# The gates' projection moved from the projection stage into the long convolution, and the late modulation rows moved the other way, in one layer of a hybrid Hyena / attention / expert block

## What is computed

```
mod_x = silu(c) @ w_mod + b_mod                    # 6 x 1024 columns; mod_c likewise for context
hx = modulate(rmsnorm(x), sh1, sc1);  hc likewise  # the first 2 x 1024 columns of mod
zx = hx @ w_in + b_in                              # 1024 x 5120
#   columns: hyena 3 x 512 | q 512 | k 512 | v 512 | gates 2 x 1024
kc, vc = hc @ w_in[k and v columns]                # context keys and values
v, x1, x2 = short_conv(hyena columns)
y = x1 * long_conv(v, filter 0);  hy = x2 * long_conv(y, filter 1)
na = neighbourhood_attention(q, k, v, kc, vc)
mix = (sigmoid(g_hy) * (hy @ w_branch_hy) + sigmoid(g_na) * (na @ w_branch_na)) @ w_out
x = x + g1 * mix                                   # the late 4 x 1024 columns of mod: g1, sh2, sc2, g2
x = x + g2 * expert_ffn(modulate(rmsnorm(x), sh2, sc2));  out = rmsnorm(x) * final_g
```

## Time and profile before

| | |
|---|---|
| median of 3 runs | 3085.92 us (3085.8, 3085.92, 3089.4) |
| the profiled execution's own time | 3089.23 us |
| its span, first to last instruction | 3087.4 us |
| mean granted TensorE clock | 0.953 of full |
| projection stage, PE's first to last matmul | 93.4 to 573.5 us |
| attention | about 578 to 829 us |
| long convolution | 829 to 1259 us |
| merge, output projection, routing | 1259 to about 1540 us |
| experts | the rest |
| busy share of the span | PE 91%, DVE 71%, ACT 50%, POOL 2% |

### The profile page before, as it was taken

The page is one execution under the profiler, slowest core; times in us unless marked ns, Lnnn a source line. Parts: engine busy times, 40 slices in busy tenths (PEclk is TensorE's granted clock), DMA queues, the critical chain, the costliest instruction groups (busy, mean ns, idle before and its releaser), DMA issues.

```text
span 3087.4 us, 34727 instructions
## 1 busy us (share of the span) xinstructions
PE 2815.9 (91%) x13273; PEld 2231.1 (72%) x13273; DVE 2180.7 (71%) x2132; ACT 1550.3 (50%) x1580; POOL 71.0 (2%) x35
## 2 busy tenths in 40 slices
PE   7899999788888994789399999999999999999997
PEld 2688888688644442568278888888888888888885
DVE  4341001376449999646698888888888988888887
ACT  4321122366421110112177777777777777777774
POOL 0000000000000000000000000000000000000000
PEclk8899999899899997899599999999999999999999
DMA  5223112522112221343399999999999999999995
GB/s 211 68 88 106 59 62 88 113 56 54 38 48 65 66 72 51 124 156 125 144 378 377 370 371 388 387 383 374 370 378 394 383 376 371 370 386 390 380 374 201
DMA packets 168042, 709.60 MB, mean 230 GB/s; under 512 B 28937, under 2 KB 66161, under 8 KB 100259
## 3 DMA queue, kind: packets, MB, share of 16 engines
q1 hardware_dynamic: 163444, 691.53, 59.3%
q0 software_dynamic: 4464, 16.25, 2.0%
HBM read 667.59 MB, written 40.14 MB: 229 GB/s over the span
## 4 chain that ended last, share of the span: by engine, by line
PE 46%; ACT 2%; issue 2%; DVE 1%; DMA 0%; DVEq 0%; ACTq 0%; POOLq 0%
PE moe_ps_gate L1827 15%; PE moe_ps_y L1817 14%; PE moe_ps_up L1827 14%; ACT moe_w_hi L1868 1%; PE moe_ps_h L1798 1%; PE moe_ps_x L1790 0%; DVE raw L1986 0%; ACT moe_xt_hi L1861 0%; DVE moe_h L1937 0%; ACT moe_sl L1879 0%; DMA moe_xe<-h_d,idx_col 0%; DVE raw L1973 0%; PE moe_ps_gate L1851 0%; PE moe_ps_gate L1853 0%; PE moe_ps_up L1851 0%
## 5 line engine op out<-in xcount | busy, mean ns | idle before, releaser
L1918 DVE TENSOR_TENSOR moe_w_lo<-raw,moe_w_hi 128x2048 fp32r<-128x2048 f32 x528 | 1207.5, 2291 | 156.9 <-ACT moe_w_hi L1868 156.9
L1868 ACT ACTIVATE moe_w_hi<-raw 128x2048 fp32r<-128x2048 f32 x528 | 1010.4, 1919 | 340.1 <-PE moe_ps_gate L1827 126.0
L1827 PE MATMUL moe_ps_gate<-moe_w_hi,moe_xt_hi 128*128 128x512 f32 (+1 forms) x768 | 288.8, 376 | 5.0 <-DVE moe_w_lo L1918 5.0
L1827 PE MATMUL moe_ps_up<-moe_w_hi,moe_xt_hi 128*128 128x512 f32 (+1 forms) x768 | 292.9, 381 | 0.0
L1827 PE MATMUL moe_ps_up<-moe_w_hi,moe_xt_lo 128*128 128x512 f32 (+1 forms) x768 | 286.6, 373 | 0.0
L1827 PE MATMUL moe_ps_up<-moe_w_lo,moe_xt_hi 128*128 128x512 f32 (+1 forms) x768 | 286.4, 373 | 0.0
L1827 PE MATMUL moe_ps_gate<-moe_w_hi,moe_xt_lo 128*128 128x512 f32 (+1 forms) x768 | 286.1, 373 | 0.0
L1827 PE MATMUL moe_ps_gate<-moe_w_lo,moe_xt_hi 128*128 128x512 f32 (+1 forms) x768 | 285.6, 372 | 0.0
L560 DVE TENSOR_TENSOR proj_w_lo<-w_in,proj_w_hi 128x2048 fp32r<-128x2048 f32 x20 | 45.7, 2290 | 275.6 <-ACT proj_w_hi L472 275.6
L1817 PE MATMUL moe_ps_y<-moe_w_hi,moe_ht_hi 128*128 128x512 f32 x704 | 218.7, 392 | 0.0
L1817 PE MATMUL moe_ps_y<-moe_w_lo,moe_ht_hi 128*128 128x512 f32 x704 | 217.1, 390 | 0.0
(11 more groups left out here) (269 smaller groups left out, 4321.9 us busy)
## 6 DMA issues: line engine op xcount, KB each, us to landing
raw<-in_w_moe SPq DMA_DIRECT2D x528, 1024.0 KB, 7.1
w_in<-in_w_in SPq DMA_DIRECT2D x20, 1024.0 KB, 5.7
hyena_w_mod<-in_w_mod SPq DMA_DIRECT2D x16, 1024.0 KB, 5.3
norm_w_mod<-in_w_mod SPq DMA_DIRECT2D x4, 2048.0 KB, 13.1
g_d<-proj_stage SPq DMA_DIRECT2D x16, 512.0 KB, 2.6
merge_gate<-g_d SPq DMA_DIRECT2D x16, 512.0 KB, 4.5
u_d<-proj_conv SPq DMA_DIRECT2D x12, 512.0 KB, 2.9
attn_k_raw<-qk_d SPq DMA_DIRECT2D x16, 320.0 KB, 6.0
```

Of the source, the lines that this page charges most:

```text
L1827: mm = pe.matmul(ps, hp[:, e % 2, k, :], wp[:, r, :], start=(k == 0 and x == 0), stop=(k == KD - 1 and x == 2))
L1868: act.activation(w_hi[:, g % PARTS], raw[:, g % RAW], ACT.Copy).then_inc(hi_ready, 1)
L1918: dve.tensor_tensor(w_lo[:, g % PARTS], raw[:, g % RAW], w_hi[:, g % PARTS].bitcast(F32), ALU.subtract).then_inc(lo_ready, 1)
```

## The change

1. **Projection.** Only 12 units are projected (hyena, q, k, v). The loops are unrolled. For the gates' 2048 columns the stage only makes the parts: 16 blocks of 128 columns are loaded (0.5 MB each), split by ACT and DVE into high and low, and stored to DRAM (`gw_d`, 1 MB each); the split input is stored too (`hq_d`, 8 transfers of 1 MB, right at the stage's start). Two blocks go with each of units 0 to 7.
2. **v** is projected for both units at once in matmuls of 512 columns for token tiles 2 to 9 (24 per tile); tiles 0 and 1 stay at 256 columns. The bias matmul goes; DVE evacuates with an addition of a bias row.
3. **Late modulation rows.** The 8 chunks are made in units 1 to 8 of the projection. For each, four quarters (0.5 MB, two slots) are loaded, and DVE folds them into one 128x512 tile with 8 operations (`fold`); one PE matmul with a column of ones sums over the partitions after the unit's own matmuls; DVE adds `b_mod` in the next unit; SP stores the row, waits for that store, and loads the next `b_mod` row into the same tile, ahead of the next quarters. Only row 0 (the latent's) is made.
4. **Long convolution.** Where `ps_mod` stood, PE runs `gates(n)`: 64 blocks (16 column blocks x 4 token quarters) of 24 fp32r matmuls of 256 columns. How many go with each of the 16 steps is a table, SHARE. POOL's queue loads the weight parts for each block anew (1 MB, two slots) and the input's quarter every 16 blocks (2 MB, one slot). ACT applies the sigmoid, SP stores 128 KB per block. The PSUM ring of `seg`/`turn`/`input` has 2 banks, not 3.
5. **Attention** stores its output to DRAM (`na_d`, 4 x 0.5 MB, the last one after the last block, with a wait), and the merge loads it (2 MB). DVE's own-step semaphores of all stages become one.

Cut to its core. SP's new order first (`chunk(u)` is u - 1 for units 1 to 8; `load_mod` waits for the fold of the quarter in its slot, `load_b_mod` for the store in `keep_mod`, `keep_mod` for the row, `keep_block` for DVE's low part), then PE's, DVE's, and the convolution's:

```diff
+                load_b_mod(0)
+                load_mod(0, 0)
+                load_mod(0, 1)
+                for q in range(T // QUARTER):
+                    for x, h in enumerate((h_hi, h_lo)):
+                        sp.dma_start(a["hq_d"][q][:, x], h[:, :, q * QUARTER:(q + 1) * QUARTER].bitcast(F32)
+                                     ).then_inc(keep["kept"], 16)
+                for u in range(SEG_V[0]):
+                    load(u + 2)
+                    n = chunk(u)
+                    if n:
+                        keep_mod(n - 1)
+                        load_b_mod(n)
+                        load_mod(n, 0)
+                        load_mod(n, 1)
+                    for c in range(CH_UNIT):
+                        if u < N_BLOCKS // 2:
+                            keep_block(2 * u + c)
+                            load_block(2 * u + c + 2)
+                        if n is not None:
+                            load_mod(n, 2 + c)
+                        keep_unit(u, c)
```

```diff
+                for u in range(SEG_V[0]):
+                    pe.wait_ge(lo_ready, u + 1)
+                    latents(u)
...
+                    if n is not None:
+                        pe.wait_ge(mod_used, 4 * n + 4)
+                        pe.wait_ge(mod_row_ready, MOD_EARLY + n)
+                        pe.matmul(ps_mod[0:1, :], ones[:], folded[:], start=True, stop=True).then_inc(mod_done, 1)
```

```diff
+                for u in range(SEG_V[0]):
+                    split(u + 1)
+                    n = chunk(u)
+                    if n:
+                        add_b_mod(n - 1)
+                    for c in range(CH_UNIT):
+                        if u < N_BLOCKS // 2:
+                            split_block(2 * u + c)
+                        if n is not None:
+                            fold(n, 2 * c)
+                            fold(n, 2 * c + 1)
+                        if u < SEG_Q[0]:
+                            convolve(u, c)
```

```diff
+        SHARE = [3, 3, 3, 3, 4, 3, 3, 3, 3, 4, 4, 4, 8, 6, 5, 5]
...
+            def _(pool):
+                for n in range(N_G):
+                    if n >= 2:
+                        pool.wait_ge(g_done, n - 1)
+                    pool.dma_start(g_parts[:, n % 2], a["gw_d"][n % N_BLOCKS]).then_inc(g_in[n % 2], 16)
+                    if n % N_BLOCKS == 0:
+                        if n:
+                            pool.wait_ge(g_done, n)
+                        pool.dma_start(h_parts[:], a["hq_d"][n // N_BLOCKS]).then_inc(h_in, 16)
...
+                def gates(n):
+                    pe.wait_ge(g_in[n % 2], 16 * (n // 2) + 16)
...
+                    for k in range(KD):
+                        for x, (w, h) in enumerate(((0, 0), (0, 1), (1, 0))):
+                            mm = pe.matmul(ps_g[:, n % 2, 0:QUARTER], g_parts[:, n % 2, w, k, :], h_parts[:, h, k, :],
+                                           start=(k == 0 and x == 0), stop=(k == KD - 1 and x == 2))
...
-                            for k in range(KD // 2):
-                                mm = pe.matmul(ps_mod[0:2, :], c_silu[:, half * KD // 2 + k, :], w_mod[:, k, :],
-                                               start=(half == 0 and k == 0), stop=(half == 1 and k == KD // 2 - 1))
+                            for n in share(NB * p + i):
+                                gates(n)
```

More of the change, by code:

```diff
@@ L57, in inc @@
         self.done += 1
+        self.step.done = self.done
     def wait(self, but=0):
@@ L463, in _ @@
+                pe.wait_ge(lo_ready, SEG_V[0] + 1)
+                bank_free(V_AT + 1)
+                values(0, 0)
+                values(1, 0)
+                pe.wait_ge(lo_ready, SEG_V[0] + 2)
+                values(0, 1)
+                values(1, 1)
+                for t in range(2, NT):
+                    bank_free(V_AT + t)
+                    values(t, None)
             @block.scalar
             def _(act):
[L465 to L472 removed]
@@ L529, in gates @@
-                def gates(i, s, last=False):
-                    u = 2 * i + s
-                    if not last:
-                        split(1 - s, SEG_G[0] // 2 + i + s, n_g + 4 * u)
-                    for c in range(CH_UNIT):
-                        b = own_bias(c, 24 + 2 * u + c, 12 + 2 * u + c + 1)
-                        act.wait_ge(stored[c], 16 * (11 + u))
-                        for th in range(2):
-                            evacuate(n_g + 4 * u + 2 * c + th, (n_g + 4 * s + 2 * c + th) % 8,
-                                     stage[:, c, th * 512:(th + 1) * 512], ACT.Sigmoid, b)
@@ L540, in _, with split @@
-                with act.Fori(0, SEG_G[1] // 2 - 1) as i:
-                    for s in range(2):
-                        gates(i, s)
-                gates(SEG_G[1] // 2 - 1, 0)
-                gates(SEG_G[1] // 2 - 1, 1, last=True)
+                def split(u):
+                    act.wait_ge(w_in[u % 2], 16 * (u // 2) + 16)
+                    if u >= 2:
+                        act.wait_ge(z_done, first_use[u - 1])
+                    act.activation(w_hi[:, u % 2], w_raw[:, u % 2], ACT.Copy).then_inc(hi_ready, 1)
@@ L691, in _ @@
                 sp.sem_inc(t_in[0], 32)
+                for j in range(PAIRS):
+                    sp.wait_ge(used, FILLS * (j + 1) + 2)
+                    sp.dma_start(a["na_d"][j], na_t[:, j, :]).then_inc(keep["kept"], 16)
+                sp.wait_ge(keep["kept"], KEPT_NA)
             @block.tensor
@@ L998, in hyena, with share @@
         PER_A = len(a_order) // PASSES
+        SHARE = [3, 3, 3, 3, 4, 3, 3, 3, 3, 4, 4, 4, 8, 6, 5, 5]
+        N_G = N_BLOCKS * T // QUARTER
+        assert sum(SHARE) == N_G and len(SHARE) == NB * PASSES
+        def share(n):
+            return range(sum(SHARE[:n]), sum(SHARE[:n + 1]))
         def split(p):
@@ L1625, in _ @@
             def _(dve):
-                dt = Tally(dve, step)
+                dt = Tally(dve, keep["dve_step"])
                 def wide(v):
```

598 lines of the change are left out of this document (320 added, 278 removed).

## The result

| | before | changed |
|---|---|---|
| median | 3087.1 us (3085.8 to 3089.4, 4 runs) | 3163.4 us (3161.0 to 3168.2, 4 runs) |
| span of the profiled execution | 3087.4 us | 3163.0 us |
| mean granted clock | 0.953 | 0.935 |

The ratio is 1.0241, with a 95% interval of 1.0229 to 1.0254. The forecast was 3101 us in a range of 3040 to 3150: the sign was right, but 3163 us lies outside the range.

The account below looks back on a forecast made before the run. PE was taken to bound the projection, DVE the convolution's passes with preparation, PE close behind. Projection -126, convolution +124, smaller things +8 and clock +9 gave +15 us: 3101 us, range 3040 to 3150.

Parts of the forecast that it names:

- PE's work in the projection, -188: Projection: gates, values and the stage's end leave PE, row sums come in; -188 us without any new wait.
- The waits in the projection, +62: Projection: PE's row sum waits between units for stores, loads and folds; +62 us, with bounds +33 and +85.
- The projection as a whole: Projection: PE's savings and the new waits together were forecast at -126 us.
- PE as the convolution's bound, +67: Convolution: with the gate blocks moved in, PE becomes the bound; 421 us against 354.2, +67 without load waits.
- The loads' waits, +57: Convolution: third and later gate blocks wait for 5.6 us loads; +32 in steps and +25 in the last pass.
- the low bound: Convolution: the case of gate loads landing in 4.4 us, which makes the convolution +99 instead of +124.
- Smaller things, +8: Attention's last store +3, POOL's 4 MB at the convolution's start +4, the merge's 2 MB load +1.
- TensorE's clock, +9: Convolution: slower clock after 12 load waits of 2.7 us, 0 to 1.8 each, 0 to 22; +9 taken.
- the first (short waits): Rival: units of 28.5 us in the projection and 4.4 us gate loads; -38, 3048 us; chance 0.28.
- the third (a real filler): Rival: hardly any new wait in projection or convolution, -113 at best, counted below -46; chance 0.05.
- waits below 113 us: Whole kernel: the border, what the sum without new waits gains; the forecast's own waits and clock were 128.
- The second: Rival: POOL's gate loads in the convolution take 7.5 us, held up by DVE products; +47, 3133 us; chance 0.15.

Follow-up runs that it names:

- p_nofold: Changed kernel without the late modulation's fold steps and `w_mod` loads, except the first chunk's first four steps and first two loads; 3098.5 us, ratio 1.0027.
- c_half: Changed kernel with each gate block's weights loaded as two 0.5 MB POOL transfers, each half waited for and released by itself; 3113.0 us, ratio 1.0071.
- c_warm2: Changed kernel with 22 useless 256-column matmuls on PE ahead of each step's third, fifth and seventh gate block; 3142.2 us, ratio 1.0169.

## Why the prediction missed

- **PE's work in the projection, -188: right.** `p_nofold` shows it: 590.2 - 412.4 = 178 with one wait of 8.5 us left, and the clock behind it. The values went from 73.6 to 54.8 us (413.5 to 468.3; 55.1 forecast).
- **The waits in the projection, +62: right in the steady units, and in the sum partly by luck.** The working's own terms add up to 64.5 (14 + 5 x 9.6 + 2.5). The runs have 63.5 us in 8 waits: 19.1 (forecast 14), then 7.5, 7.8, 8.1, 7.4 and 5.3 (9.6 each), 0.4 (2.5) and 7.9 in unit 8 (none). The steady unit took 31.3 to 33.6 us (32.3 forecast). The chain was the one described: the row's store, then `b_mod`, the quarters of `w_mod` each behind other transfers on SP, the folds. Unit 8, which the forecast held free, had a wait of its own. On SP its last quarter stands behind the store of the first key block, and that store waits until the context's product is evacuated too:
```profile
375.82 0.35 SPq L425 DMA_DIRECT2D qk_d<-proj_stage  x1
376.21 0.43 SPq L405 DMA_DIRECT2D proj_w_mod<-in_w_mod  x1
381.21 1.54 DVE L615 SCALAR_TENSOR_TENSOR proj_folded<-proj_w_mod,c_silu,proj_folded 128x512 f32<-128x512 f32 x2 [17.64 <-DMA proj_w_mod<-in_w_mod]
382.86 1.87 PE L518 MATMUL proj_ps_mod<-proj_folded,proj_ones 128*1 128x512 f32 x2 [7.94 <-DVEq L621]
```
- **The projection as a whole gained 108, not 126.** 16 us (188 - 63.5 - 108.1) are nowhere in the sum. They are slower matmuls: seven of the eight waits leave PE at the lower clock for the row sum (1.87 us instead of 1.02) and the first matmuls of the next unit, and PE's busy time is 14.3 us above that of `p_nofold`, which has one such wait itself. How much of this a faster PE would give back is not shown. From the first row sum to the sixth the five units took 162.8 us against 117.1 in `p_nofold`, 45.7 more where 48 was forecast, slow matmuls and all: there the chain may set the length whatever PE's clock is. Counted by units, 13 of the missing 18 us are the first wait (5) and unit 8 (8).
- **PE as the convolution's bound, +67: right.** +62.9 with the loads taken out, with the idle at a pass's end still there (in the changed kernel 9.31 us before `seg`, then 9.33 for it, against the 10.59 and 9.15 of the earlier trace rows).
- **The loads' waits, +57: too small.** 71.6 us of idle PE. The landing was right (5.7 us against 5.6 taken), but the wait is 3.0 to 3.25 us, not 2.7: POOL's issue comes after the block's end, and the wait at block 48 took 5.1 us; the profile names no releaser there, but in `c_half` the same wait is for the token quarter's load. By the fit in the Trainium skill, "DMA: Bandwidth & Descriptors", section "Anatomy of one DMA — SWDGE (gpsimd) path", such a transfer would take 4.4 us, an estimate; by it the waits would have been near the low bound, and the trace disagrees, with no landing under 5.5 us.
- **Smaller things, +8: +13.6** (3.1 + 10.1 + 0.4), the excess being the late decay at the convolution's start.
- **TensorE's clock, +9: the step that failed.** The text said that the 12 waits of 2.7 cost "0 to 1.8 each, 0 to 22: I take +9". It counted the waits of the passes with preparation alone. Left out were the last pass, where pairs after a wait take 7.3 to 7.9 us instead of 6.1, and the projection, where the earlier trace rows were read at full clock for every unit. In the convolution the runs show 27 us (what `c_warm2` gets back) to 36 (107.2 less the 71.6 of waits). In the projection PE was slower by some 16 us, of which no run shows how much the time paid.

So the term that was most mis-sized is the clock in the convolution. Against the forecast's +15: clock in the convolution +18 to +27, slower matmuls in the projection +16, load waits +15, smaller things +6, projection waits +1 or +2, PE's convolution work -4. With the upper figure that gives the measured +76.

Of the rivals, the first (short waits) and the third (a real filler) needed waits below 113 us; they were 135 before any clock. The second came near the convolution's loss (+165 against +170) for the wrong reason. Its mechanism, loads of 7.5 us held up by DVE's products, did not occur: the loads landed in 5.7 us in the median, 5.5 at the soonest, with DVE busy for 255.9 of 386.6 us. By the Trainium skill, "SBUF — State Buffer", section "SBUF: two separate sides", a DVE operation with two SBUF inputs holds off only GpSimd work that reads SBUF; the trace agrees, as the landings show.

## What to carry to other kernels

Price a wait on TensorE together with the matmuls behind it: here a wait of 3 us could add 1.3 to 2.4 us of half-clock work, and in the convolution these small prices came to 27 to 36 of the 107 us that the loads cost. When work is moved to be a filler, count the slots of its operands: with two slots of one block each, the third block waits for a whole landing less one block, and halving the transfer unit, with the same bytes and the same room, took away half of that. An instruction that ends another engine's chain, like a row sum on PE, is better placed later than between two units: half a unit later, with its row's store, gave 30 us here, though a chain longer than a unit still made it wait.

## What the runs showed of the hardware that was not expected

- Idle times of the same length cost differently: behind 3.19 us the block took 3.14 us, behind 3.16 us in the same pass 5.49. What PE did before differs, and no run here settles which of it matters.
- Twenty-two useless matmuls in each of the 21 waits make the kernel 21 us faster, though no load lands sooner for it.
- POOL's transfers of 0.5 MB did not land sooner in the median than those of 1 MB (6.0 against 5.7 us; the soonest 4.0 against 5.5), probably because two or more were under way; so the gain came from their earlier issue and release.
- The attention, which no experiment edits, took between 239 and 251 us in the traces. A difference of up to 12 us that lies there in one trace says nothing.
